# Twenty-four unread matmuls around the broadcast of each sublayer's output norm

## The reference

```python
def rms_norm(x, g):
    xf = x.astype(jnp.float32)
    y = xf * lax.rsqrt(jnp.mean(xf * xf, axis=-1, keepdims=True) + EPS)
    return (y * g.astype(jnp.float32)).astype(x.dtype)

def half_ffn(x, g_pre, g_post, w_in, w_out):
    gate, up = jnp.split(rms_norm(x, g_pre) @ w_in, 2, axis=-1)
    return x + 0.5 * rms_norm((jax.nn.silu(gate) * up) @ w_out, g_post)
...
        xp = xp + rms_norm(yp, g[3])
```

## Time and profile before

| | before |
|---|---|
| median of 3 runs | 2374.9 us |
| lowest, highest | 2373.54, 2384.54 us |
| span of the profiled execution | 2375.1 us |
| its mean granted TensorE clock | 0.955 of full speed |
| TensorE busy (matmul) | 2213.7 us, 93% |
| VectorE, ScalarE, GpSimd busy | 61%, 40%, 7% |

### The profile page before, as it was taken

One profiled execution on the slowest core, in us unless ns is written; L12 is line 12 of the kernel. 1 busy time (PEld: TensorE's weight loads), 2 busy tenths in 40 slices (PEclk: granted clock), 3 DMA queues, 4 the chain that ended last, 5 costly groups with the idle time before them and its releaser, 6 DMA issues.

```text
span 2375.1 us, 41971 instructions
## 1 busy us (share of the span) xinstructions
PE 2213.7 (93%) x17475; PEld 2129.9 (90%) x17475; DVE 1457.4 (61%) x1727; ACT 941.8 (40%) x1111; POOL 158.0 (7%) x214
## 2 busy tenths in 40 slices
PE   7999989999999979899999999779999999998997
PEld 6999989998998945789989998468999999898997
DVE  5665866646655567366656645655664665686663
ACT  3443344444434335244344434324443444433442
POOL 3001010001001000010010001001000000101000
PEclk9999999999999989889999999979999999898998
DMA  6554445553554434245545554414554555354550
GB/s 204 177 196 142 160 144 163 185 201 125 177 195 136 161 113 142 89 142 178 188 131 178 186 188 141 143 45 127 183 189 149 166 185 187 118 178 133 185 188 28
DMA packets 286121, 370.76 MB, mean 156 GB/s; under 512 B 12247, under 2 KB 212360, under 8 KB 285924
## 3 DMA queue, kind: packets, MB, share of 16 engines
q1 hardware_dynamic: 282378, 364.57, 46.0%
q10 hardware_dynamic: 3610, 4.28, 0.5%
HBM read 364.87 MB, written 8.11 MB: 157 GB/s over the span
## 4 chain that ended last, share of the span: by engine, by line
PE 56%; DVE 5%; POOL 1%; issue 1%; ACT 0%; ACTq 0%; DVEq 0%; POOLq 0%
PE ps L1371 15%; PE ps L1373 15%; PE ps L1372 15%; PE ps L1423 1%; PE ps L1424 1%; PE ps L1427 1%; PE ps L1677 1%; POOL rs L609 1%; PE ps L1590 1%; DVE kt_dec L1176 1%; DVE probs L1123 1%; PE ps L1547 1%; PE ps L1580 1%; PE ps L1379 1%; PE ps L1390 1%
## 5 line engine op out<-in xcount | busy, mean ns | idle before, releaser
L1371 PE MATMUL ps<-x_hi,w_high_ring 128*128 128x264 f32 x3112 | 893.8, 287 | 0.0
L860 DVE TENSOR_TENSOR w_low_ring<-wstage,w_high_ring 128x2048 fp32r<-128x2048 f32 x332 | 728.4, 2228 | 262.7 <-ACT w_high_ring L630 184.2
L1373 PE MATMUL ps<-x_hi,w_low_ring 128*128 128x264 f32 x3112 | 889.2, 286 | 0.0
L1372 PE MATMUL ps<-x_lo,w_high_ring 128*128 128x264 f32 x3112 | 888.2, 285 | 0.0
L1372 PEld LDWEIGHTS ps<-x_lo,w_high_ring 128*128 128x128 f32 x3112 | 592.8, 190 | 0.0
L1371 PEld LDWEIGHTS ps<-x_hi,w_high_ring 128*128 128x128 f32 x3112 | 591.3, 190 | 0.8 <-issue 0.2
L1373 PEld LDWEIGHTS ps<-x_hi,w_low_ring 128*128 128x128 f32 x3112 | 591.5, 190 | 0.0
L1371 PE MATMUL ps<-h_hi,w_high_ring 128*128 128x264 f32 x1664 | 474.4, 285 | 4.1 <-issue 4.1
L1373 PE MATMUL ps<-h_hi,w_low_ring 128*128 128x264 f32 x1664 | 474.9, 285 | 0.0
L1372 PE MATMUL ps<-h_lo,w_high_ring 128*128 128x264 f32 x1664 | 473.2, 284 | 0.0
L630 ACT ACTIVATE w_high_ring<-wstage 128x2048 fp32r<-128x2048 f32 (+2 forms) x172 | 307.1, 1816 | 311.6 <-PE ps L1373 299.7
(11 more groups left out here) (287 smaller groups left out, 1898.5 us busy)
## 6 DMA issues: line engine op xcount, KB each, us to landing
wstage<-in_ffn_w_in_dram SPq DMA_DIRECT2D x352, 512.0 KB, 5.0
wstage<-in_ffn_w_out_dram SPq DMA_DIRECT2D x160, 512.0 KB, 4.6
wstage<-in_conv_w_in_dram SPq DMA_DIRECT2D x48, 512.0 KB, 4.9
wstage<-in_nsa_w_in_dram SPq DMA_DIRECT2D x20, 512.0 KB, 4.8
wstage<-in_ffn_w_out_dram SPq DMA_DIRECT2D x32, 256.0 KB, 3.3
wstage<-in_conv_w_out_dram SPq DMA_DIRECT2D x16, 512.0 KB, 4.8
wstage<-in_cache_nsa_dram SPq DMA_DIRECT2D x16, 512.0 KB, 4.6
wstage<-in_diff_w_in_dram SPq DMA_DIRECT2D x16, 512.0 KB, 4.9
```

The costliest lines, as they stand in the source:

```text
L860: V.tensor_tensor(w_low_ring[:, u % RING, 0:n, 0:cols], wstage[:, stage_of["w", u] % RING, 0:n, 0:cols], w_high_ring[:, u % RING, 0:n, 0:c ...
L1371: MM(out, wh, hi, start=first, stop=False)
L1372: MM(out, wh, lo, start=False, stop=False)
L1373: return MM(out, wl, hi, start=False, stop=last)
```

## The change

A new helper issues `count` matmuls that multiply the bf16 identity by the 256 columns of the constant mask `own_cmp`, into a bank of PSUM which nobody reads before it is overwritten. It is called twice at the end of each sublayer: 13 times ahead of the broadcast, behind a wait on ScalarE's copies, and 11 times behind it.

```diff
+            def keep_running(bank, count):
+
+                for _ in range(count):
+                    MM(ps[:, bank, 0:256], ident_b[:, :], own_cmp[:, :, :].rearrange("p j n -> p (j n)"),
+                       start=True, stop=True, skip_group_check=True)
+
...
                 pe.wait_ge(y_squared, (GT + 1) * (s.i + 1))
                 norm_stats(2 * s.i + 1, sq[:, NC - 1, :], first=False)
+                pe.wait_ge(y_copied, GT * s.i + 3)
+                keep_running(4 * s.outs[1].set + 1, 13)
                 norm_bcast(2 * s.i + 1)
+                keep_running(4 * s.outs[1].set + 1, 11)
                 if s.kind == "conv":
```

## The result

The changed kernel takes 2348.5 us (median of 4 runs, 2344.4 to 2351.7) against 2374.5 us (4 runs). The ratio is 0.989, 95% interval 0.986 to 0.992. Timed once more beside fresh runs of the kernel before it took 2350.0 us (5 runs, 2348.1 to 2351.2), ratio 0.991 (0.989 to 0.993). The forecast was 2354 us, range 2345 to 2367.

The account below looks back on a forecast made before the run. TensorE, busy 93% of the span and partly at half clock, was taken as the bound. Gains of 16.0, 3.2 and 2.0 us at the boundaries summed to 21.2, taking 2375.1 us to 2354, range 2345 to 2367.

Parts of the forecast that it names:

- The bound and the slack: Sublayer boundaries: TensorE bounds; L904's start sets everything later, and VectorE's slack before it caps the products' gain at 1.33 us.
- Plain boundaries: Boundaries not behind a convolution: 0.66 us from the broadcast plus 1.33 from products, 2.0 us at each of eight, 16.0 together.
- The ninth: The remaining boundary not behind a convolution, 9.6 us at half speed: gain 0.66 + 2.60, rounded down to 3.2 us.
- The price of one: One added matmul in the boundary waits: 0.12 us, bounds 0.115 and 0.195; thirteen and eleven cost 0 at full clock.
- The clock is held: Sublayer boundaries: with added matmuls at work for 1.56 and 1.32 us of the two waits, the clock stays at 1.00.
- The convolutions: Two boundaries behind a convolution: added work and better clock cancel up to the transposes; 1.0 us gained each, bounds 0 and 1.9.
- in most cases: Behind the convolution's transposes, TensorE's unfilled 2.44 us wait for `x_hi` lets the clock fall mostly, so half is gained.
- The norm before: Other norm of each sublayer, 2.12 us wait left unfilled: five of twelve falls now, about 2.9 us per fall.
- more than seven slow stretches behind the norms before: Sign of being wrong in the changed profile: this many would take the gain back elsewhere.
- the fall moves to the norm before: Rival, chance 0.05: all twelve unfilled waits there see falls, seven more cost 20 us, gain gone, 2375 us.
- The sum: Whole kernel: 16.0 + 3.2 + 2.0 = 21.2 us gained, taken from the profiled span of 2375.1 us, giving 2354 us.

Follow-up runs that it names:

- The 26: Changed kernel with 26 instead of 13 added matmuls ahead of the sublayer-end broadcast, 11 behind as before; 2366.4 us.
- both norms filled: Changed kernel plus 13 more added matmuls ahead of the broadcast of each sublayer's other norm, in its wait for the power; 2335.4 us.
- all these waits filled: Changed kernel plus 13 matmuls ahead of the other norm's broadcast, and the 11 moved behind the transposes at the two convolutions; 2331.1 us.

## Why the prediction held, step by step

**The bound and the slack: right.** L904 was where everything hung. Plain boundaries were forecast at 15.3 us and measured 15.23 to 15.25 in all nine, with VectorE's idle time gone. The ninth, forecast to give 3.2 us, came to the same 15.25 us from 18.55 (3.3 us). In sum 19.2 us were forecast and 20.0 measured. That all nine are now equal to 0.02 us is the sign of an engine that the clock doesn't touch: VectorE's chain.

**The price of one: right, a little high.** 0.12 us was taken, 0.110 measured. Both waits covered them. The 26, at the same price, overran the wait and were 0.95 us late.

**The clock is held: right**, and shown by undoing it: with one call alone, with narrow ones or with half as many it fell at every one of the eleven boundaries; with full-width work over most of both waits it fell at none of the nine plain ones, in seven traces.

**The convolutions: the mis-sized term.** I took 1.0 us each, because I expected the clock to fall in the wait behind the transposes "in most cases". It gave 1.9 and 2.0 us, the upper bound of 1.9 that I had given and a little over, because the clock did not fall there in either trace of the changed kernel. That bound came from the slow products; VectorE's slack, which I read at the plain boundaries only, caps the gain here too: its idle time in front of L904 was 1.56 and 1.90 us before and is nothing now. The other half of the step was right: the transposes end 3.2 us behind the start of the broadcast. But the fall is real elsewhere: with both norms filled, or with the 26, it came at one of the two, and without the eleven at both. So what failed is "in most cases": with the eleven ahead of the transposes it fell at 2 of 10 such places, in five traces. The 1.04 us of transposes may well be work for the clock, as the run with transposes of full tiles suggests (these have 18 rows of output), and I had treated them as next to nothing.

**The norm before: the right rival, in a form that I had not seen.** I had priced a long fall at 2.9 us and taken five falls as unchanged. I had also named more than seven slow stretches behind the norms before as a sign of being wrong, and there were nine. The wait there is 2.12 us in eleven sublayers, but 3.39 us in the first, which I had counted with the others. The stretches from L904 to the next sublayer-end broadcast show prices directly; before and changed (columns as in rows 3):

```profile
352.35:543.30 190.95, 186.86 (x1507) 186.15 (x1507) 114.42 (x97) 75.76 (x64) 4.46 (x6) 0.98 0.55 182
560.65:748.64 187.99, 183.90 (x1506) 183.24 (x1506) 114.34 (x97) 75.74 (x64) 4.46 (x6) 1.00 0.55 184
```

```profile
554.54:744.01 189.47, 186.98 (x1520) 186.01 (x1520) 114.42 (x98) 75.73 (x64) 4.46 (x6) 0.99 0.55 183
351.30:539.29 187.99, 185.50 (x1519) 184.54 (x1520) 114.36 (x98) 75.76 (x64) 4.46 (x6) 1.00 0.57 185
```

Without a fall the stretch of a feed-forward sublayer is 187.99 us in either kernel. The fall of before costs 2.96 us, the one of the changed kernel 1.48. The changed kernel had more falls, nine for five, but all except the first sublayer's were short: over the eleven later sublayers eight at 1.2 to 1.6 us for three at 3.0 and one at 1.2. The two lots came out nearly alike, and the rival ("the fall moves to the norm before") happened in number and not in price. That they were short is luck, as no row of before said it: the kernel with the 13 alone had nine in the later sublayers, five of them 6.8 us long, and its middle is 2128.5 us, 9 us more than that of the changed kernel. The prediction also put nothing down for the falls inside the attentions, which alone moved a sublayer by 9 us in the kernel with half as many.

**The sum.** 21.2 us forecast, 23.9 measured at the boundaries and 25.3 in the span: 0.8 more at plain boundaries, 1.9 at the convolutions, and 1.4 from what I had left at zero. The forecast also took the span of before as one scale with the times of runs, and in the changed kernel a time stands 1.9 us above its span. The range and the sign were right; that the part outside the boundaries came out near zero is luck as much as foresight.

## What to carry to other kernels

When an engine with a variable clock is the bound, read the clock column of the stretch behind each of its waits: the loss is not in the wait but in the work behind it, and removing it is worth only as much as the next engine's slack there. Unread work is free until it meets the signal that the engine waits for; past it every piece is paid in full, so count pieces against the wait. Where the engine already holds the inputs of something that another engine waits for, as here the transposes, put the unread work behind it. A change that shifts all times also redraws where the clock falls elsewhere, so compare several executions, or sum the trace by stretches, before crediting the change with a total.

## What the runs showed of the hardware

- At the ends of the sublayers of the kernel before the granted clock fell in or just behind waits of 1.76 and 1.77 us with only the sums ahead of them and the broadcast between them; with narrow matmuls in them it fell with 1.3 to 1.4 us of idle time left in each. It did not always fall at once: in the kernel with the 13 alone it fell 1.4 us into a full stream of products, 3.2 us behind the end of the last broadcast matmul.
- Float32 transposes of full tiles held the clock as well as bf16 matmuls of twice the columns.
- One program's executions spread by up to 0.8% (the kernel before from 2364.3 to 2380.8 us in 25 runs, 0.7%; that with the 13 alone from 2356.3 to 2374.8 in ten), that with all these waits filled by 0.07% (2329.7 to 2331.2 in four; the one with both norms filled still had one of four at 2343.9). The time goes with the mean granted clock of the same execution: over the 25 of the kernel before the correlation is -0.95, from 0.961 in the fastest to 0.953 in the slowest. So the spread is mostly that of the time at half speed; where in the program it differs is seen in traces only.
